# Expert slots in rounds 1 to 7 read from a scattered DRAM table, with empty slots left out of the row fetch

## What is computed

```
g_idx = argmax(xt @ w_rg + b_rg)                    # one group per token
top_p, top_i = top_k(softmax(e_logits of g_idx), 2) # two experts of the group
weights = p_g * top_p / sum(top_p)
for each expert e, for the tokens that chose it:
    y[token] += weight * ((silu(xb @ w_gate_e[e]) * (xb @ w_up_e[e])) @ w_down_e[e])
```

## Time and profile before

| | |
|---|---|
| median of the runs | 1619.0 us |
| the profiled execution | 1618.77 us |
| span of its profile | 1617.0 us |
| PE busy, share of the span | 1580.7 us, 98% |
| DVE, ACT, POOL busy | 52%, 36%, 34% |
| HBM read | 230.59 MB |

### The profile page before, as it was taken

The page is one execution under the profiler, slowest core; times in us unless marked ns, Lnnn a source line. Parts: engine busy times, 40 slices in busy tenths (PEclk is TensorE's granted clock), DMA queues, the critical chain, the costliest instruction groups (busy, mean ns, idle before and its releaser), DMA issues.

```text
span 1617.0 us, 19949 instructions
## 1 busy us (share of the span) xinstructions
PE 1580.7 (98%) x7386; PEld 1197.5 (74%) x7386; DVE 841.6 (52%) x1419; ACT 583.0 (36%) x955; POOL 547.3 (34%) x239
## 2 busy tenths in 40 slices
PE   7999999999999999999999999999999999999997
PEld 6888779887888888887876768888877885444543
DVE  6447586135744466245777786344243654433434
ACT  4227455243322234415532342343243333112213
POOL 4441227622444435840432124455424410000000
PEclk9999999999999999999999999999999989999998
DMA  5331224522333333630322113344313449999991
GB/s 190 103 92 40 78 92 143 154 68 84 92 92 104 92 91 109 185 102 24 99 72 68 37 52 95 103 122 128 103 52 92 149 185 372 419 423 422 421 418 72
DMA packets 52786, 235.93 MB, mean 146 GB/s; under 512 B 6240, under 2 KB 7136, under 8 KB 48096
## 3 DMA queue, kind: packets, MB, share of 16 engines
q1 hardware_dynamic: 48960, 222.60, 40.0%
q0 software_dynamic: 2016, 7.34, 1.1%
q10 hardware_dynamic: 1728, 4.87, 0.9%
HBM read 230.59 MB, written 4.19 MB: 145 GB/s over the span
## 4 chain that ended last, share of the span: by engine, by line
PE 92%; DVE 5%; issue 1%; ACT 1%; DMA 0%; SPq 0%; DVEq 0%; ACTq 0%
PE G L1821 72%; PE O L1821 7%; PE S L1821 6%; PE TR L1821 5%; PE TR L1932 2%; PE G L2391 1%; DVE sq L1084 1%; DVE U L1055 1%; DVE sumsq L1019 0%; DVE U L1798 0%; DVE arena L1442 0%; DMA w_ring<-in_stream_dram 0%; ACT cm_hi L595 0%; DVE sumsq L1728 0%; DVE RB L1390 0%
## 5 line engine op out<-in xcount | busy, mean ns | idle before, releaser
L544 POOL TENSOR_TENSOR lo_ring<-w_ring,hi_ring 128x1024 fp32r<-128x1024 f32 x219 | 533.6, 2438 | 770.9 <-ACT hi_ring L579 770.8
L579 ACT ACTIVATE hi_ring<-w_ring 128x1024 fp32r<-128x1024 f32 x219 | 231.4, 1058 | 564.2 <-PE G L1821 560.7
L1821 PE MATMUL G<-xa_hi,hi_ring 128*128 128x512 f32 x928 | 375.6, 405 | 9.6 <-DVE xa_lo L1146 9.0
L1821 PE MATMUL G<-xa_hi,lo_ring 128*128 128x512 f32 x928 | 362.6, 391 | 0.0
L1821 PE MATMUL G<-xa_lo,hi_ring 128*128 128x512 f32 x928 | 362.3, 390 | 0.0
L1821 PEld LDWEIGHTS G<-xa_hi,hi_ring 128*128 128x128 f32 x928 | 175.1, 189 | 48.0 <-issue 11.9
L1821 PEld LDWEIGHTS G<-xa_lo,hi_ring 128*128 128x128 f32 x928 | 175.2, 189 | 37.7 <-issue 2.4
L1821 PEld LDWEIGHTS G<-xa_hi,lo_ring 128*128 128x128 f32 x928 | 174.8, 188 | 37.2
L1821 PE MATMUL G<-yb_hi,hi_ring 128*128 128x512 f32 x388 | 153.1, 395 | 0.0
L1821 PE MATMUL G<-yb_hi,lo_ring 128*128 128x512 f32 x388 | 151.1, 389 | 0.0
L1821 PE MATMUL G<-yb_lo,hi_ring 128*128 128x512 f32 x388 | 151.0, 389 | 0.0
(11 more groups left out here) (351 smaller groups left out, 2494.4 us busy)
## 6 DMA issues: line engine op xcount, KB each, us to landing
w_ring<-in_stream_dram SPq DMA_DIRECT2D x219, 512.0 KB, 3.5
arena<-in_w_gu_dram SPq DMA_DIRECT2D x16, 2048.0 KB, 12.3
ex_rings<-in_w_dn_dram SPq DMA_DIRECT2D x40, 512.0 KB, 16.1
ex_low<-in_w_gu_dram SPq DMA_DIRECT2D x8, 2048.0 KB, 18.7
ex_rings<-in_w_gu_dram SPq DMA_DIRECT2D x8, 2048.0 KB, 16.3
arena<-in_w_dn_dram SPq DMA_DIRECT2D x16, 512.0 KB, 14.6
sq<-in_w_dn_dram SPq DMA_DIRECT2D x8, 512.0 KB, 18.6
X<-in_x_in_dram SPq DMA_DIRECT2D x8, 256.0 KB, 5.4
```

The source lines that it names most:

```text
L544: nc.gpsimd.tensor_tensor(lo_ring[:, s, :], w_ring[:, s, :], hi_ring[:, s, :], ALU.subtract).then_inc(low, 1)
L579: nc.scalar.activation(hi_ring[:, m % RING, :], w_ring[:, m % RING, :], ACT.Copy).then_inc(high, 1)
L1821: return nc.tensor.matmul(*args, **kw)
```

## The change

For quads 2 to 7 the slot numbers and weights no longer come from selection products. Instead:

- A DRAM table `slot_info` has 512 places of 8 bytes (a number and a weight) for each of the 32 experts. In the conv stage, DVE clears an SBUF tile and ACT writes it over the table (128 x 1 KB).
- In the router tail DVE works out for each token the two places in the table (expert x 512 + rank) and lays its number (minus 1024) and weight beside them. POOL first issues the row fetch of quad 1, then 8 indirect DMAs that each scatter 128 entries of 8 bytes, waits until they have landed, and issues two DMAs that read the round's part of the table, 64 partitions x 16 pairs x 8 bytes each, into the tile `slot_info`. It issues the row fetch of quads 2 to 7 after that.
- In each quad `table_tokens` (two DVE instructions) takes the next quad's numbers from that tile. `select_rows`, `slots_of` and the reading of their products are gone from quads 1 to 6. DVE waits once for the table, behind quad 0.
- An empty slot now has index 1024, which is beyond the bound that the fetch is given (511), so that its row is not fetched. The row tile keeps what it held there, with weight 0.

```diff
+        slot_dram = nc.dram_tensor("slot_info", (EXPERTS * T, 2), F32, kind="Internal").ap()
+        slots_by_expert = slot_dram.rearrange("(a e r s) c -> e r s a c", e=2, r=ROUNDS, s=SLOTS)
...
-                    nc.gpsimd.indirect_dma_start(slot_rows[p], None, token_rows, where).then_inc(rows_land[p], 16)
+                    nc.gpsimd.indirect_dma_start(slot_rows[p], None, token_rows, where, bounds_check=T - 1,
+                                                 oob_is_err=False).then_inc(rows_land[p], 16)
...
-            with pool.Fori(1, QUADS) as it:
+            fetch_rows(1)
+            pool.wait_ge(cleared, 16)
+            pool.wait_ge(own_rows, 4)
+            for c in range(2):
+                for t in range(TT):
+                    where = bass.IndirectOffsetOnAxis(own_index[:, c * TT + t:c * TT + t + 1], 0)
+                    k = 2 * (2 * t + c)
+                    nc.gpsimd.indirect_dma_start(slot_dram, where, own_info[:, k:k + 2], None).then_inc(own_sent, 16)
+            pool.wait_ge(own_sent, 16 * 2 * TT)
+            for e in range(2):
+                nc.gpsimd.dma_start(slot_info[e * SLOTS:(e + 1) * SLOTS, :, :],
+                                    slots_by_expert[e][0:1].rearrange("r s a c -> (r s) a c")).then_inc(tab_land, 16)
+            with pool.Fori(2, QUADS) as it:
                 fetch_rows(it)
...
+                if f == 0:
+                    act.wait_ge(zeros_up, 1)
+                    act.dma_start(slot_dram.rearrange("(p r) c -> p (r c)", p=P), zeros).then_inc(cleared, 16)
...
+            nc.vector.memset(zeros, 0.0).then_inc(zeros_up, 1)
...
+            do(nc.vector.tensor_tensor(r_t[6], S[:, 1, 0:P].rearrange("p (t e) -> p t e", t=TT),
+                                       row_base.unsqueeze(1).broadcast_to([P, TT, EXPERTS]), ALU.add))
+            for c, mine in enumerate((r_t[7], r_t[3])):
+                note(nc.vector.tensor_tensor(mine, r_t[6], r_t[4 + c], ALU.mult))
+            settle()
+            for c, mine in enumerate((r_t[7], r_t[3])):
+                note(nc.vector.tensor_reduce(own_at[:, c, :], mine, AX.X, ALU.add))
+            settle()
+            nc.vector.tensor_scalar(own_index, own_at.rearrange("p c t -> p (c t)"), 0.0, 0.0, ALU.add,
+                                    ALU.max).then_inc(own_rows, 1)
             dve.wait_ge(rt_e, 2)
...
+            nc.vector.tensor_copy(own_fields[:, :, :, 0], slot_table[:, 0, :, 0:6:5]).then_inc(own_rows, 1)
...
+            def table_tokens(r):
+
+                info = slot_info[:, bass.ds(r * 2, 2), :]
+                nc.vector.tensor_scalar(slot_token, info[:, :, 0], float(AWAY), None, ALU.add).then_inc(ix_ready, 1)
+                nc.vector.tensor_copy(nxt.rearrange("p (f a) -> p a f", f=2), info).then_inc(nx_ready, 3)
...
                 if not primed:
                     current(it)
-                    if more:
-                        select_rows(it + 1, r + 1)
-                        slot_tokens(it + 1, slots_in[1])
                 hidden(0)
+                if more and not primed:
+                    table_tokens(r + 1)
...
                 quad(first, 0, before=False, primed=isinstance(rd, int))
+                if isinstance(rd, int):
+                    dve.wait_ge(tab_land, 32)
                 with dve.Fori(1, QUADS - 1) as r:
...
                 gate_up(it, 0)
-                if more and not primed:
-                    slots_of(it + 1, r + 1)
                 if before:
                     scatter(it - 1, 4, KT)
...
-                if more:
-                    pe.wait_ge(ix_ready, it + 1)
-                    pe.wait_ge(nx_ready, it * 3 + 6)
+                if primed:
+                    pe.wait_ge(ix_ready, 1)
+                    pe.wait_ge(nx_ready, 6)
```

More of the change, by code:

```diff
@@ L43 @@
 HALF_LINE = 16
+AWAY = 2 * T
 VECTORS = {}
@@ L263, in build @@
         cur_ready = sem("current_slots_ready")
-        slots_up = sem("slots_moved")
+        cleared = sem("slot_rows_cleared")
+        zeros_up = sem("zeros_ready")
+        own_rows = sem("slot_rows_known")
+        own_sent = sem("slot_rows_scattered")
+        tab_land = sem("slot_rows_read")
         ga_full = sem("gathered")
@@ L399, in build @@
         token_rows = nc.dram_tensor("token_rows", (T, D), F32, kind="Internal").ap()
+        slot_dram = nc.dram_tensor("slot_info", (EXPERTS * T, 2), F32, kind="Internal").ap()
+        slots_by_expert = slot_dram.rearrange("(a e r s) c -> e r s a c", e=2, r=ROUNDS, s=SLOTS)
+        zeros = A(8192, 2 * P)
+        row_base = A(1696, EXPERTS)
+        own_at = A(11186, 2, TT)
+        own_index = A(11194, 2 * TT).bitcast(U32)
+        own_info = A(11202, 4 * TT)
+        own_fields = own_info.rearrange("p (t c f) -> p t c f", t=TT, c=2)
+        slot_info = A(11218, 2 * PAIRS).rearrange("p (a f) -> p a f", f=2)
         row32 = [U[:, 2 * t:2 * t + 2, :].rearrange("p a c -> p (a c)") for t in range(TT)]
@@ L523, in _ @@
                 with sp.Fori(1, ROUNDS) as rd:
+                    sp.wait_ge(nx_ready, rd * (3 * QUADS))
+                    for e in range(2):
+                        sp.dma_start(slot_info[e * SLOTS:(e + 1) * SLOTS, :, :],
+                                     slots_by_expert[e][bass.ds(rd, 1)].rearrange("r s a c -> (r s) a c")
+                                     ).then_inc(tab_land, 16)
                     with sp.Fori(0, PAIRS // 2) as q:
@@ L1581, in _ @@
                     note(nc.vector.tensor_scalar(r_iota64, r_iota, -64.0, None, ALU.add))
+                    note(nc.vector.tensor_scalar(row_base, r_iota, float(T), None, ALU.mult))
                     nc.vector.memset(counts[:, 0:1], 0.0).then_inc(x_add, KT)
@@ L1659, in _ @@
             dve.wait_ge(row_up, 1)
-            select_rows(1, 1)
+            ids = slot_id[:, 0:SLOTS].unsqueeze(1).unsqueeze(1).broadcast_to([P, TT, 4, SLOTS])
+            places = rank[:, :, 4:8].unsqueeze(3).broadcast_to([P, TT, 4, SLOTS])
+            nc.vector.tensor_tensor(sel.rearrange("p t (e s) -> p t e s", e=4), places, ids,
+                                    ALU.is_equal).then_inc(sel_done, 1)
             dve.wait_ge(rk_all, 1)
@@ L1670, in _ @@
             do(nc.vector.reciprocal(r_s[11], r_s[10]))
[L1671 to L1674, removed]
+            weights = [own_fields[:, :, c, 1] for c in range(2)]
+            nc.vector.tensor_tensor(weights[0], r_s[11], r_s[3], ALU.mult).then_inc(own_rows, 1)
+            dve.wait_ge(own_rows, 2)
+            nc.vector.tensor_tensor(weights[1], weights[0], r_s[9], ALU.mult).then_inc(own_rows, 1)
+            dve.wait_ge(own_rows, 3)
+            for c in range(2):
+                do(nc.vector.tensor_tensor(r_t[4 + c], r_t[4 + c], spread(weights[c], EXPERTS), ALU.mult))
             do(nc.vector.tensor_tensor(wc, r_t[4], r_t[5], ALU.add))
@@ L1769, in round_of @@
                 if not isinstance(rd, int):
-                    select_rows(first, 0)
-                    slot_tokens(first, slots_in[1])
+                    dve.wait_ge(tab_land, rd * 32 + 32)
+                    table_tokens(0)
                 gathered(first)
@@ L2468, in round_of @@
                 if not isinstance(rd, int):
[L2469 to L2472, removed]
                     for half in range(2):
```

19 lines of the change are left out of this document (4 added, 15 removed).

## The result

The changed kernel takes 1629.05 us against 1619.01 us before; the ratio is 1.0056, with a 95% interval of 1.0046 to 1.0067. It is slower by 10 us. 1614.4 us and a gain were forecast; the time lies inside the range, on its slow side. One of the changed kernel's six executions took 5669.08 us, for a reason that nothing on record shows, and is left out of the ratio. The profiled execution took 1628.92 us, with a span of 1626.6 us, 9.6 us more than before.

The account below looks back on a forecast made before the run. PE was taken to bound a quad, with DMA close behind. 1618.8 - 5.5 (slot products) + 0.85 (later start of quad 0) = 1614.2, and 0.2 for the median gave 1614.4 us; range 1612 to 1637.

Parts of the forecast that it names:

- the slot products: On PE's path between O and S in quads 1 to 6: removing them saves 0.91 us each, 5.5 us in all.
- Leaving out the empties: In a quad's row fetches: half of the 2048 slots are not fetched, saving 1.1 to 1.25 us of transfers a quad.
- DVE's new instructions in the router tail: Six instructions ahead of L1667 take 1.55 us, 0.72 hidden in DVE's idle time, so quad 0 starts 0.85 us later.
- The scatters are all in by about 1363: Behind quad 1's fetch: the last scatter starts at about 1356.8, and a DMA's fixed time is 4.9 us.
- 1376: 4 us before it is needed, at no cost: DVE's wait behind quad 0: the table lands between 1370 and 1383, middle 1376, and is needed by about 1380.4.
- the gap ahead of quad 0: Rival: TensorE's clock falls in the 1.1 us gap and narrow products there, costing 5 us, 1619; in a 0.2 group.
- The small pieces wait their turn one by one: Rival, table DMAs: each 8-byte piece takes one turn among weight rows; table lands near 1403, 1637 us; chance 0.33.
- its milder form: Only the scatters' pieces take single turns among weight rows: the table lands at 1386 to 1396, 1620 to 1630 us.
- POOL's issues would be stretched where DVE copies: Around POOL's ten DMAs: DVE's two-port modes lock GpSimd out, moving the table's landing later by up to a few us.
- The empty slots are still moved: Rival, row fetches: DMA needs 32.5 us a quad against PE's 31.3, giving 1616.5 us; in a group with chance 0.2.
- The likeliest case: Whole kernel: the table lands in time and the gain shows, 1612.5 to 1616.5 us; chance 0.47.

Follow-up runs that it names:

- the two kernels whose table is laid out otherwise: The whole changed kernel with 64-byte table rows, 1613.66 us, and the whole changed kernel with its table laid out by slot, 1613.93 us.
- the table by slot: The whole changed kernel with a slot's 16 pairs side by side in the table, read back in 128-byte pieces: 1613.93 us.

## Why the prediction was wrong

**What held.** PE bounded a quad, and the slot products were worth 0.9 us each: the issues of `ex_low` are now 31.3 to 31.7 us apart, and 31.3 throughout with neither scatters nor read-back.

```profile
1520.14 0.33 SPq L487 DMA_DIRECT2D ex_low<-in_w_gu_dram  x1
1551.46 0.50 SPq L487 DMA_DIRECT2D ex_low<-in_w_gu_dram  x1
```

Leaving out the empties brought DMA below that and gave nothing by itself. DVE's new instructions in the router tail, 1.55 us by the prediction, are here with a wait between them:

```profile
1337.78 0.28 DVE L1699 TENSOR_TENSOR arena<-S,arena 128x128 f32<-128x128 f32 x1
1338.10 0.49 DVE L1702 TENSOR_TENSOR arena<-arena 128x128 f32<-128x128 f32 x2
1338.63 0.48 DVE L1705 TENSOR_REDUCE arena<-arena 128x4 f32<-128x128 f32 x2
1339.15 0.17 DVE L1707 TENSOR_SCALAR arena<-arena 128x8 uint32<-128x8 f32 x1
1339.23 0.16 DVE L1710 TENSOR_REDUCE arena<-arena 128x4 f32<-128x16 f32 x1
```

L1710, the old L1667, starts at 1339.23 for 1338.43: +0.80 us, 0.85 forecast. This part of the sum is what the kernel with neither scatters nor read-back takes: 1613.56 us for 1614.4.

**The step that failed** is "The scatters are all in by about 1363", and with it "1376: 4 us before it is needed, at no cost". The scatters were in at 1374.6, 12 us later, and the table was in SBUF at 1392.3 for 1376. The cause is not in the prediction's steps at all: I asked how long the small DMAs would wait behind the weights, and never how long the weights would wait behind them. The sum had no term for the stream. That term is 10.9 us up to 1376 us (0.6 of it without any of the table's DMAs), and it came back as 4.8 us of waiting ahead of quad 1. The late table gave 4.2 us of waiting in quad 1. To both stops belongs the clock, which I had put only to the gap ahead of quad 0: 0.92 and 0.83 granted from 1360 to 1400 us. Quad 1's 16 pairs of products from `ex_low`, 7.0 us before, took 9.9 (1377.68 to 1387.55), and the eight products of the scatter behind the second stop 3.4 us (1393.84 to 1397.28) for 2.0, half of the 3.94 in the earlier trace rows: 4.4 us together. The two waits and the clock are 13.4 of the 15.1 us by which the span is above that of the kernel with neither (1626.6 - 1611.5); I have not split the other 1.7.

**The rivals.** "The small pieces wait their turn one by one" gave 1620 to 1630 for its milder form, the table at 1386 to 1396, and both numbers were met, for another reason. That the time lies in the range is luck: the range was stretched that far for this rival alone, and its mechanism is refuted. POOL's queue moved 2016 packets without the table's DMAs, 2272 with the eight scatters and 2336 with the read-back too:

```profile
q0 software_dynamic: 2336, 3.72, 0.9%
```

A row fetch counts 2016 / 14 = 144 packets, its 128 rows and one that closes for each of 16 DMA engines. A scatter counts 32, where single turns would make 144 of it as well; so 8 pieces share a packet. And 64-byte pieces, which are as many, cost nothing. The packet rule quoted in the prediction from the Trainium skill, *DMA: Bandwidth & Descriptors*, section "Queues, rings and completion order", agrees with these counts. It is silent on how long a packet of small writes takes, and that was the question. That POOL's issues would be stretched where DVE copies did not show: all eight scatters took 0.96 to 1.02 us to issue. It is a weak test, as DVE was busy for only 1.4 of the 10 us from 1348 to 1358. "The empty slots are still moved" is refuted by 3.72 MB for 7.34. TensorE's clock did fall, as a consequence and later than that rival had it.

The likeliest case's own range, 1612.5 to 1616.5, holds the two kernels whose table is laid out otherwise; theirs landed at about 1375 and 1372 us, for the 1376 of the forecast. The forecast held for the idea with other addresses in the table, and failed for the kernel as it is.

## What to carry to other kernels

A DMA that is small in bytes can be large for its neighbours: before small writes or reads are put beside a full stream, ask what they take from it, as well as when they land. In the profile, look for a DMA share that stays while GB/s falls. Three layouts were cheap here: pieces of 32 bytes or more, 8 bytes in rows 64 bytes apart, and 8 bytes side by side in the table by slot, whose writes spread over the remainders of 4096 (with stretches of 4352 bytes, which spread them too, 4.2 us of time were still lost). Dear was 8 bytes side by side in many stretches that start 4096 bytes apart. Where the stream is the next bound, a us lost there is not caught up.

## What the runs showed that I had not expected

- Eight scatters of 1 KB each cost the stream more than 9 us. In the run without the read-back (windows below) the 4 us from 1356 on moved 127 GB/s, with a DMA share of 1.31 and 0.80. Less the 0.6 us that the run without both shows as well, and divided by eight, a scatter costs the stream 1.2 us with rows 8 bytes apart in stretches of 4096 bytes, 0.3 with stretches of 4352, 0.2 with slots 64 or 4096 bytes apart, and nothing that shows with pieces of 32 bytes or more.

```profile
1352.00:1356.00 4.00, 4.00 (x21) 1.44 (x22) 0.54 (x1) 0.38 (x1) 3.09 (x4) 1.00 1.31 278
1356.00:1360.00 4.00, 4.00 (x22) 1.35 (x20) 0.42 (x1) 0.38 (x1) 1.10 (x2) 1.00 0.80 127
```

- SP stood in the issue of one DMA for 12.2 us and in a group of five for 13.5 while the DMA engines were behind; before, the same entries took 2.0 and 3.8 us. The load queued behind them was issued at 1391.75, 4 us after PE's last product from its buffer (1387.6), where before it was issued 0.2 us after.
- 8-byte reads from stretches 4096 bytes apart can cost the stream too: 5.4 us were lost with two such DMAs in one execution, while the median of the time rose by 0.7 us. What decides it stays open. The read-back landed in 13.2 us in the changed kernel, in 8.5 with 8 bytes out of 64-byte rows and in 5.8 with pieces of 128 bytes.
